# A hybrid decoder step on one core: second buffers for the scan's states, the low halves of the weights formed one unit ahead, and prompt attention in steps of four half units

## The reference

```python
mod = silu(c) @ w_ada + b_ada; shift, scale, gate = split(mod, 3)
h = rmsnorm(x, g_pre) * (1 + scale) + shift
q, k, v, z_a, z_b, xbc, dt_raw, r_a, r_b = split(h @ w_in)
# A: dilated window attention, groups (128,1), (512,4), (2048,16), 8 heads x 128
#    prompt: banded windows; decode: keys and values gathered from the caches
o_a = softmax over the groups' log-sum-exps of the group outputs
p_a = (o_a * silu(z_a)) @ w_o_a
# B: causal conv of width 4 on xbc, then the Mamba-2 scan in chunks of 128
#    (8 groups, 32 heads of 64, state 128), D skip, gate silu(z_b), grouped rmsnorm
p_b = yn @ w_o_b
out = (sigmoid(r_a) * p_a + sigmoid(r_b) * p_b) @ w_o
y = x + gate * rmsnorm(out, g_post)
# also returned: new key/value windows, conv rows and scan states
```

## Time and profile before

| | |
|---|---|
| median of 3 executions | 3415.59 us (3413.01 to 3420.86) |
| the profiled execution's own time | 3431.45 us |
| its span in the trace | 3429.7 us |
| mean granted TensorE clock | 0.944 of full speed |
| PE busy | 3095.8 us, 90% of the span |
| VectorE busy | 1978.9 us, 58% |
| GpSimd busy | 1103.1 us, 32% |
| ScalarE busy | 867.8 us, 25% |
| DMA traffic | 704.94 MB, mean 206 GB/s |

### The profile page before, as it was taken

The page is one execution under the profiler, slowest core; times in us unless marked ns, Lnnn a source line. Parts: engine busy times, 40 slices in busy tenths (PEclk is TensorE's granted clock), DMA queues, the critical chain, the costliest instruction groups (busy, mean ns, idle before and its releaser), DMA issues. The chain is left out here.

```text
span 3429.7 us, 53566 instructions
## 1 busy us (share of the span) xinstructions
PE 3095.8 (90%) x23404; PEld 2985.7 (87%) x23404; DVE 1978.9 (58%) x1996; ACT 867.8 (25%) x1045; POOL 1103.1 (32%) x367
## 2 busy tenths in 40 slices
PE   5799999999999999989997988898887889999995
PEld 4698999899999999979996978887887878899995
DVE  3201799788857778777866466656646655211204
ACT  2111122232232222222231322322322232211221
POOL 0123333233323332233332333423324333333331
PEclk7799999999999999999998999999998989999998
DMA  8777777453537675555664455345445445766533
GB/s 304 258 260 262 304 277 254 162 198 119 172 129 256 233 266 193 194 229 207 250 230 168 176 192 176 134 175 210 155 161 203 170 148 179 266 248 243 212 137 111
DMA packets 222256, 704.94 MB, mean 206 GB/s; under 512 B 28659, under 2 KB 131819, under 8 KB 172459
## 3 DMA queue, kind: packets, MB, share of 16 engines
q1 hardware_dynamic: 159478, 471.33, 39.4%
q0 software_dynamic: 5248, 174.60, 12.6%
q10 hardware_dynamic: 57296, 55.59, 4.8%
HBM read 630.85 MB, written 245.17 MB: 255 GB/s over the span
## 5 line engine op out<-in xcount | busy, mean ns | idle before, releaser
L1156 PE MATMUL acc<-act,w_hi 128*128 128x288 f32 (+1 forms) x6432 | 1962.9, 305 | 141.8 <-POOL w_lo L779 134.0
L1157 PE MATMUL acc<-act,w_hi 128*128 128x288 f32 (+1 forms) x6432 | 1922.3, 299 | 0.0
L1158 PE MATMUL acc<-act,w_lo 128*128 128x288 f32 (+1 forms) x6432 | 1920.9, 299 | 0.0
L779 POOL TENSOR_TENSOR w_lo<-w_raw,w_hi 128x2048 fp32r<-128x2048 f32 (+1 forms) x209 | 968.8, 4636 | 1859.5 <-ACT w_hi L821 1844.1
L1156 PEld LDWEIGHTS acc<-act,w_hi 128*128 128x128 f32 (+1 forms) x6432 | 1233.2, 192 | 174.7 <-POOL w_lo L779 138.3
L1157 PEld LDWEIGHTS acc<-act,w_hi 128*128 128x128 f32 (+1 forms) x6432 | 1233.2, 192 | 2.8
L1158 PEld LDWEIGHTS acc<-act,w_lo 128*128 128x128 f32 (+1 forms) x6432 | 1230.4, 191 | 0.9
L821 ACT ACTIVATE w_hi<-w_raw 128x2048 fp32r<-128x2048 f32 (+1 forms) x209 | 384.1, 1838 | 407.6 <-PE acc L1158 235.4
L1517 DVE TENSOR_TENSOR side<-side 128x2048 f32<-128x2048 f32 x96 | 279.6, 2913 | 150.0 <-DMA side<-in_vals_t 142.1
L1488 DVE TENSOR_TENSOR side<-side 128x2048 f32<-128x2048 f32 x96 | 308.7, 3216 | 83.1 <-DMA side<-in_keys_t 79.0
L887 ACT ACTIVATE ev<-acc 128x576 f32<-128x576 f32 x160 | 103.7, 648 | 893.3 <-PE acc L1158 889.9
(11 more groups left out here) (232 smaller groups left out, 2077.9 us busy)
## 6 DMA issues: line engine op xcount, KB each, us to landing
w_raw<-in_w_in_t SPq DMA_DIRECT2D x160, 1024.0 KB, 8.0
out_s_kv<-in_cache_a_w POOLq DMA_DIRECT2D x80, 1632.0 KB, 9.0
side<-in_keys_t SPq DMA_DIRECT2D x52, 1024.0 KB, 7.7
side<-in_vals_t SPq DMA_DIRECT2D x52, 1024.0 KB, 8.3
w_raw<-in_w_ada_t SPq DMA_DIRECT2D x48, 1024.0 KB, 7.7
out_s_kv<-in_cache_a_w POOLq DMA_DIRECT2D x24, 1344.0 KB, 8.3
w_raw<-in_w_o_b_t SPq DMA_DIRECT2D x16, 1024.0 KB, 7.6
w_raw<-in_w_o_t SPq DMA_DIRECT2D x16, 1024.0 KB, 8.7
```

The costliest lines, as they stand in the source:

```text
L779: nc.gpsimd.tensor_tensor(wl[:, u % 2, 0:kt, 0:cols], raw[:, s % 3, 0:kt, 0:cols], wh[:, u % 2, 0:kt, 0:cols].bitcast(F32), ALU.subtract). ...
L1156: nc.tensor.matmul(out, wh[:, c, k, 0:cols], high, start=(k == 0), stop=False)
L1157: nc.tensor.matmul(out, wh[:, c, k, 0:cols], low, start=False, stop=False)
L1158: mm = nc.tensor.matmul(out, wl[:, c, k, 0:cols], high, start=False, stop=(k == kt - 1))
```

## The change

1. *Prologue.* The small vectors are loaded ahead of the `w_ada` tiles, PE turns them (`vectors`) after the second tile, the weights of unit 0 are fetched ahead of the last two `w_ada` tiles, and unit 0 waits for its activations step by step.
2. *POOL.* `w_lo(u+1)` is issued ahead of the copy and the scan's parts of unit u.
3. *Slots.* Units 111 to 164 use two slots for weights instead of three. The third slot holds a second `h0` and two more `h0T` (in the last group these lie in `xa_free`, another free region). The scan's loads are placed anew: carried states at o = 3, 5, 7, 9, decode states at o = 4 and 8, stores at o = 12 and 18. SP's lag behind the units is shorter (`seen`).
4. *Side work.* Grains are placed 8 to 7 halves instead of 17 to 16 (`grain_half`), `value_news` one token to a half over nine halves, a step of prompt attention takes four halves (`PACE`). `SOFT0`, `VALS0`, `NEWS0`, `NEWV0` and `FOLD0` move from 113, 117, 208, 217 and 223 to 107, 111, 196, 209 and 218.
5. *Output.* The gate is multiplied in where the output leaves PSUM, the squares are taken unit by unit from PSUM on ACT, and the tail is one DVE operation `out * rstd + x` for each of four tiles; the tile of the decode rows is scaled on ACT and added on POOL.

The diff, cut to its core:

```diff
-SLOT_OF = {entry: NADA + i for i, entry in enumerate(STREAM)}
+ADA_SLOT = [n if n < NADA - 2 else n + 1 for n in range(NADA)]
...
+    _few = _kind == "u" and BLOCK0 <= _n < A0 + 4
+    if _few:
+        _slot = _next[1] % 2
+        _next[1] += 1
+    else:
+        _slot = _next[0] % 3
+        _next[0] += 1
...
+PACE = 4
...
 def grain_half(n):
 
-    return n * 16 // 17
+    return n * 7 // 8
 
...
 VALS0 = SOFT0 + 4
 NEWS0 = VALS0 + grain_half(NGR) + 1
-NEWV0 = NEWS0 + 9
-FOLD0 = NEWV0 + 6
+NEWV0 = NEWS0 + 13
+FOLD0 = NEWV0 + 9
...
-        h0T = side[:, 7936:8448]
+        spare = raw[:, 2, :, :].rearrange("p k n -> p (k n)")
         St = side[:, 8448:8704]
         lastm = side[0:SAMP, 8704:8736].rearrange("p (h b) -> p h b", h=4)
...
+        xa_free = side[:, 11232:13536]
+
+        def h0(g, j):
+
+            buf = (xa_free if g == SG - 1 else spare)[:, 0:1024] if j else side[:, 6912:7936]
+            return buf.rearrange("p (b n) -> p b n", b=NB)
...
+
+            i = hT_buf(g, k)
+            return (xa_free if g == SG - 1 else spare)[:, 512 + 512 * i:1024 + 512 * i] if i else side[:, 7936:8448]
+
         X, Y, Z = (ps_t, ps_w), ps_s[:, 0:512], ps_s[:, 512:1024]
...
+                    if s == SLOT_THIRD:
+                        sp.wait_ge(yt, 5 * (SG - 1))
+                        sp.wait_ge(s_out, 32 * (SG - 1))
...
+                if n == NADA - 2:
+                    weights(0)
...
+            def spare_free(g, i):
+
+                if g == 0 and i:
+                    sp.wait_ge(lo, ENTRY[THIRD_LAST][1] + 1)
+                if g == SG - 1 and i:
+                    sp.wait_ge(a_lo, SPLIT_OA + 4)
+
+            def carried(g, k):
+
+                older = [(gg, kk) for gg in range(g + 1) for kk in range(4) if (gg, kk) < (g, k) and hT_buf(gg, kk) == hT_buf(g, k)]
+                if older:
+                    sp.wait_ge(yt, 5 * older[-1][0] + older[-1][1] + 1)
+                spare_free(g, hT_buf(g, k))
+                sp.dma_start(h0T(g, k), A["state_t"][g, k]).then_inc(hT_in[hT_buf(g, k)], 16)
...
-                sp.dma_start(h0, A["state_ssm"][0, :, 4 * g + 2 * j:4 * g + 2 * j + 2].rearrange("b h p n -> (h p) b n")).then_inc(h0_in, 16)
+                after(sp, s_out, 16 * (2 * g + j - 1))
+                spare_free(g, j)
...
-                if o in (4, 8, 10, 12):
-                    k = (4, 8, 10, 12).index(o)
-                    after(sp, yt, 5 * g + (k if k else -1))
-                    sp.dma_start(h0T, A["state_t"][g, k]).then_inc(hT_in, 16)
-                if o == 4 and g == 0:
+                if o in (3, 5, 7, 9):
+                    carried(g, o // 2 - 1)
+                if o == 4:
                     old_states(g, 0)
-                if o == 11:
+                if o == 8:
+                    old_states(g, 1)
+                if o == 12:
                     new_states(g, 0)
-                    sp.wait_ge(s_out, 16 * (2 * g + 1))
-                    old_states(g, 1)
-                if o == 17:
+                if o == 18:
                     new_states(g, 1)
-                    if g + 1 < SG:
...
             def seen(u):
 
-                return max(0, 2 * min(u, NGATE + 2) - 4, 2 * u - (8 if u < A0 + 3 else 4))
+                lag = 8 if u < BLOCK0 else 6 if u < A0 + 2 else 2 if u < A0 + 4 else 4
...
+            weights_low(0)
+            for u in range(NU):
+                if u + 1 < NU:
+                    weights_low(u + 1)
                 if 1 <= u < 11 or 85 <= u < A0 or B0 <= u:
...
-                            pool.wait_ge(lo, u + 1)
+                            pool.wait_ge(lo, min(u + 2, NU))
...
+            pool.wait_ge(f_s, 1)
+            pool.wait_ge(c_in, 80)
+            nc.gpsimd.tensor_tensor(outs[4][0:SAMP, :], outs[4][0:SAMP, :], xT[4][0:SAMP, :], ALU.add).then_inc(f_p, 1)
...
-            def squares(q):
-
-                act_e.wait_ge(o_c, 8 * q + 8)
+            def squares(v):
+
...
+            nc.scalar.activation(outs[4][0:SAMP, :], outs[4][0:SAMP, :], ACT.Copy, scale=fstat[0:SAMP, 4, 2:3]).then_inc(f_s, 1)
...
+                    if n == 1:
+                        vectors()
...
+            def value_news(t):
+
...
-                if half == NEWV0:
-                    value_news()
+                if NEWV0 <= half <= NEWV0 + NT:
+                    value_news(half - NEWV0)
...
-                TC(outP[:, :, cols], src.rearrange("p (t c) -> p t c", t=4)).then_inc(o_c, 1)
-                TC(outs[4][0:SAMP, cols], smp).then_inc(o_c, 1)
+                if v == 0:
+                    dve.wait_ge(gg_d, 2)
+                TT(outP[:, :, cols], src.rearrange("p (t c) -> p t c", t=4), gateP[:, cols].unsqueeze(1).broadcast_to((P, 4, P)),
...
-                gg = gateP if t < 4 else gateS
-                STT(outs[t][0:n, :], outs[t][0:n, :], fstat[0:n, t, 2:3], gg[0:n, :], ALU.mult, ALU.mult).then_inc(f_s, 1)
-                dve.wait_ge(f_s, t + 1)
...
-                TT(outs[t][0:n, :], outs[t][0:n, :], xT[t][0:n, :], ALU.add).then_inc(f_d, 1)
+                STT(outs[t], outs[t], fstat[:, t, 2:3], xT[t], ALU.mult, ALU.add).then_inc(f_d, 1)
```

More of the change, by code:

```diff
@@ L1150, in multiply @@
                 sl = slice(half * HALF, (half + 1) * HALF)
-                first = {A0: SPLIT_OA, B0: SPLIT_Y, O0: SPLIT_M}.get(u) if half == 0 else None
+                first = {0: 0, A0: SPLIT_OA, B0: SPLIT_Y, O0: SPLIT_M}.get(u) if half == 0 else None
                 for k in range(kt):
-                    if first:
+                    if first is not None:
                         pe.wait_ge(a_lo, first + k + 1)
```

383 lines of the change are left out of this document (207 added, 176 removed).

## The result

The median fell from 3418.23 to **3315.70 us** (four executions of each kernel; the 3415.59 above is that of the first three), a ratio of 0.970 (95% interval 0.968 to 0.972). That is faster, as forecast, and inside the range, but 44 us above the predicted 3272. The profiled execution took 3314.87 us (span 3313.1), 116.6 less than the one of before.

The account below looks back on a forecast made before the run. PE bounds the kernel (90% of the span), with half of what can be won in the scan stage's waits and clock. Terms -120 - 15 - 4.5 + 3 - 8 = -144.5 give 3287 us, times 0.9954 a median of 3272; range 3205 to 3345.

Parts of the forecast that it names:

- Scan stage, -120: Units 111 to 160: 93.6 us of PE's waits for `w_lo` and carried states go, plus 26 from a higher clock.
- Rival C: Scan stage: the new order on POOL changes nothing, 61.7 us of `w_lo` waits stay; 3333 us; chance 0.10.
- D: Scan stage: with two slots SP stands at stores, weights come late, the gain is lost; about 3545 us; chance 0.05.
- B: Scan stage: POOL and DVE exclude each other, a group needs 117 us, the stage gains 26; 3365 us; chance 0.10.
- Decode and attention, -15: Decode and prompt attention stages: -24 for PE's wait for DVE, +19 crowding, -10 other gaps; ends -45 and +10.
- the prediction's own sign of being wrong: The forecast is wrong if the two stages before the scan stage together take over 1275 us.
- the price of crowding: Decode and attention: cost of denser grains and attention steps on DVE at 87% load, 0 to 35 us, taken as 19.
- Rival A: Attention on a crowded DVE: each of 32 steps, in odd halves, costs a late `w_lo` of 2.5 us; 3309 us; chance 0.18.
- Units 0 to 30, 0: POOL order in q and k units: `w_lo` waits there are POOL behind ACT, so 0 us, ends -5 and +5.
- Prologue, -4.5: Before unit 0: a DMA hole of 5 us closes, `w_lo` comes earlier, two tiles some 3 us later; ends -9 and +2.
- A units, +3: Output projections: SP waits at A0 for activations to be split, ahead of needed loads; +3 us, ends -5 and +13.
- Tail, -8: Tail: ten DVE operations become four, 13.8 us, less 2 for later squares and 4 for POOL's addition; ends -5 and -12.

Follow-up runs that it names:

- experiment 7: The changed kernel with the old order on POOL: each unit's `w_lo` behind the copy and scan work of the unit before; 3394.10 us.
- experiment 8: The kernel before with only the new POOL order, `w_lo(u+1)` ahead of unit u's copy and scan work; three slots, single buffers; 3288.56 us.
- experiment 4: The changed kernel with prompt attention begun one half later (`ATT0` 62 for 61), so each step falls in an even half; 3271.58 us.
- experiment 5: The changed kernel with the attention step moved ahead of the decode grains in DVE's program of each half; 3226.56 us.
- experiment 1: The changed kernel with all side work as before: attention steps of five halves, grains 17 to 16, newest values in one half; 3284.74 us.
- experiment 2: The changed kernel with attention steps of four halves kept, but grains 17 to 16 and the newest values in one half; 3297.35 us.
- experiment 6: As experiment 1 (steps of five halves, grains 17 to 16), but with the newest values spread over nine halves; 3257.06 us.
- experiment 11: Experiment 2 (steps of four halves, grains 17 to 16, newest values in one half) with the attention step ahead of the grains on DVE; 3211.39 us.
- experiment 12: Experiment 11 with prompt attention begun one half later, in even halves (`ATT0 = 62`); 3198.35 us.
- experiment 3: The changed kernel with attention steps of five halves again; grains 8 to 7 and newest values over nine halves stay; 3332.56 us.
- experiment 9: The changed kernel with a single buffer for the carried states, loaded at the old places; 3349.40 us.
- experiment 10: The changed kernel with a single buffer for the decode states, each load behind the landed store, at the old places; 3326.70 us.

## Why the prediction was right, and where it was off

*The sum.* The parts came to -144.5 in the forecast and to -116.6 in the profiled executions, 28 us apart. The other 16 of the 44 us come from the last step: the forecast took the median to stand at 0.9954 of a profiled execution, since it had before, and after it stood at 1.0003 (3315.70/3314.87). One profiled execution's distance to the median does not carry over to another kernel. Against the runs of before, 3413 to 3427 us, the profiled one was simply a long one. That the total came as near as 44 us is partly luck: the middle missed by 33 us, and the scan stage and the prologue, better than forecast by 12.5 and 4.9, covered half of it.

*Scan stage, -120.* -132.5, right in size, and the clock did as said: 0.92 to 0.98, PE's busy time 34 us less (26 taken, 51 the bound). Residual waits were near the 3 us a group assumed, for DVE (21.7 us in units 117 to 160). But the account of who earned it was wrong. The prediction led it back to the store that the load had to see landed. The runs show that POOL's queue order earned 118.6 us alone, that three carried buffers are worth 28 beside it (the parts overlap and don't add up to the 132.1), and that the second decode buffer is worth nothing that can be told from scatter: with `w_lo(u+1)` ahead of it the scaling is not in anybody's way, and its waits for the load fell from 251.5 to 15.1 us by themselves. The term's size was right because the edits were priced together. The chain names the late load and the in-order queue behind it; either would have done, and the queue was the cheaper.

*Rival C* (the order changes nothing) is refuted by experiments 7 and 8. *D* (two slots starve the row) did not come, as no wait for `w_lo` is left in units 117 to 160; but the chain of experiment 7 shows something like it, SP standing at a slot, once the order on POOL is the old one. *B* (POOL and DVE exclude each other) is refuted by a group of 102 us where it said 117. The rule behind B shows in single operations all the same: the mean of the convolution's products rose from 1319 ns (L1688 before) to 1788 and the small copy's fell from 1214 (L1677) to 521, as other operations now stand beside `w_lo`. In both traces a product that overlaps no operation of POOL takes 0.75 us, and one that does takes 3.7 to 3.8 in the mean; 18 of the 96 are of the second kind before and 34 after. In the tail 4.1 us were lost beside 4.62 of POOL. The Trainium skill (GPSIMD Engine Reference, Key points) names contention with GpSimd for VectorE instructions with two SBUF inputs; the traces agree, for the products and the operation of the tail are of that kind. The small copy has one input, and no row tells in what mode it ran. Rival B's sum was too strict and its mechanism right.

*Decode and attention, -15.* This is the step that failed; it came to +18, and with 1287.7 us for the two stages the prediction's own sign of being wrong (over 1275) is there. The 24.1 us went as said, and DVE's load was as worked out (6.4 us busy a half, 6.5 forecast). What failed was the price of crowding, "between 0 and 35 us", taken as 19: units 31 to 95 took 67 us more (63.7 and 3.3), against 49 won in units 96 to 110, where 34 were forecast. (The forecast's own terms, -24, 0 to 35 and -5 to -20, end at -44 and +6, not at its -45 and +10.) The price was worked out from DVE's share, as though 87% left room enough; what counts is where the maximum stands in DVE's queue and what stands behind exp in ACT's. Rival A, given 0.18, named the mechanism, exp waiting for the maximum in all 32 steps (303.0 us) and `w_lo` late behind it, and the odd halves too, but without their weight: experiment 4 prices them at 44 us, experiment 5 the order on DVE at 89. That its +22.5 is near the +18 is partly luck. It charged 80 us of waits for `w_lo` and 44.1 came, it expected DVE over 85% busy where units 31 to 79 have 75%, and of the +18 only 4.4 are idle time of PE, the rest its longer busy time, of which A says nothing.

*Units 0 to 30, 0.* +8.4. The q units are 4.2 us longer and the k and z units before unit 31 also 4.2. Both are the density's, whose grains begin in unit 11: with 17 to 16 again (experiments 1, 2, 6, 11 and 12) units 0 to 30 take 443.1 to 448.8 us, where they took 447.0 before, and with 8 to 7 in steps from half 61 (the change, experiments 3, 5, 7, 9 and 10) 454.1 to 456.5.

*Prologue, -4.5.* -9.4. From 20 to 30 us the DMA engines are now busy in 98% of their time, so the hole of 5 us is closed. Unit 0 still starts only as its `w_lo` is done, but the `w_hi` for it begins at 126.43 us and not at 135.80, 2.2 us ahead of the last split of activations where it came 0.6 behind. That makes 2.8 us and the hole 5. Whether the 3 us set against them, for two `w_ada` tiles pushed back, came or not can't be told: the experiments with this same prologue took 128.4 to 134.8 us for it, and experiment 8 with the old one 136.1 where the kernel before took 142.4, so one pair of profiled executions does not fix such a term to 3 us.

*A units, +3,* came to +5.1 in the profiled pair (134.9 to 140.0), but the order on POOL by itself takes these units down to 129.7 (experiment 8), and the kernels with two slots have 140.0 to 145.4. So the rest of the change costs 10 us or more here, and which part of it does so is not shown. *Tail, -8,* came to -6.2. The addition on POOL cost the 4.1 us said, the squares about 0.5 and not 2. What was left out is the output: from DVE's last operation to the end 9.1 us go by (3304.05 to 3313.1), where 6.1 did before (3423.6 to 3429.7), probably since the tiles now follow each other faster than before.

## What to carry to other kernels

In an in-order queue ask of each blocking instruction what stands directly behind it, and put what the busiest engine needs ahead of what may wait: two such moves, of a few lines, won more here (119 us in their stage and 89 us in all) than all second buffers. An engine at 85% of its time can be harmless and one at 74% hold the others up, by order alone. And when the period of some side work changes, look at which slot of the main loop it now falls into: five halves alternated between a good and a bad place, four hit the bad one each time.

## What was not expected of the hardware

PE's granted clock (1 is full speed) rose in units 117 to 160 from 0.91 to 0.98 when its gaps of up to 9.6 us went. For the same work, the units 117 to 160, PE was busy 753.68 us before and 723.01 after, while its idle time fell from 124.4 to 23.0 us. So 101 us of gaps cost 31 us more in slower multiplies, about a third on top of their length. Experiment 7, with 75 us of idle time, stands between (748.38 at 0.94), though for its 52 us of gaps over the change it pays 25, about half. Around the wait of 24.1 us the clock was lower still; unit 110 before, from its start to that of the next:

```profile
1818.70:1859.10 40.40, 16.31 (x110) 13.47 (x109) 30.19 (x16) 2.57 (x2) 7.64 (x2) 0.70 0.24 88
```
